# A hybrid encoder layer on one core: two more paired weight tiles, the first head's keys and values among them, the gates' chain in fewer places, the steps nine pieces earlier, and seven vector additions handed to adding transfers

## The reference

```python
xn = rmsnorm(x)
q, k, v, o, ig, fg, u, gates = split(xn @ w_in)      # 8200 output columns
# branch A: 4 heads x 256, chunks of 64 tokens
ig = ig + b_i;  lf = log_sigmoid(fg + b_f)
for each chunk: bcum = cumsum(lf); m_tok = running max; w = exp(logd - m_tok)
    s = (q @ k.T) * w;  num = s @ v + inter * (q @ C);  C = decay * C + (w_last * k).T @ v
ya = (rmsnorm(h) * sigmoid(o)) @ w_proj_a
# branch B
c = causal_dwconv(u[:, :1024] * sigmoid(u[:, 1024:]), width 31)
yb = silu(layernorm(c)) @ w_proj_b                   # mean and variance over all 1024 channels
x = x + rmsnorm((sigmoid(g_A) * ya + sigmoid(g_B) * yb) @ w_out)
x = x + rmsnorm(ffn(x))                              # up, conv of width 3, gelu, down
```

## Time and profile before

| | before |
|---|---|
| median of 3 runs | 1919.84 us (1919.48 to 1921.33) |
| profiled execution | 1919.55 us |
| its span, first to last instruction | 1917.8 us |
| mean granted clock | 0.996 |
| PE busy | 1889.2 us, 99% of the span |
| DVE busy | 1355.3 us, 71% |
| ACT busy | 859.7 us, 45% |
| POOL busy | 84.9 us, 4% |

### The profile page before, as it was taken

How to read it: one execution, slowest core, us unless ns; L and a number is a source line. 1 busy time by engine, 2 the same in 40 slices (tenths; PEclk the granted TensorE clock), 3 DMA queues, 4 the chain that set the end, 5 groups by cost and what they waited for, 6 DMA issues and landing times.

```text
span 1917.8 us, 33091 instructions
## 1 busy us (share of the span) xinstructions
PE 1889.2 (99%) x13241; PEld 1864.8 (97%) x13241; DVE 1355.3 (71%) x2078; ACT 859.7 (45%) x1609; POOL 84.9 (4%) x136
## 2 busy tenths in 40 slices
PE   9999999999998999999999999999999999999997
PEld 8999999999998999999999999999999999999997
DVE  7798999899997646664444468976777676646363
ACT  5554444444424556542122355654454444635342
POOL 0010001000111111110000000000000000000000
PEclk9999999999999999999999999999999999999999
DMA  3445445455354645559131323221222122556654
GB/s 134 141 119 138 135 131 148 109 159 183 103 141 124 192 129 176 153 153 346 45 138 44 127 74 106 90 80 68 86 72 80 68 90 102 190 196 213 208 173 153
DMA packets 117031, 255.09 MB, mean 133 GB/s; under 512 B 19980, under 2 KB 59660, under 8 KB 116880
## 3 DMA queue, kind: packets, MB, share of 16 engines
q1 hardware_dynamic: 105936, 223.10, 33.9%
q0 software_dynamic: 10944, 29.89, 8.1%
HBM read 191.44 MB, written 61.51 MB: 132 GB/s over the span
## 4 chain that ended last, share of the span: by engine, by line
PE 86%; DVE 11%; issue 1%; ACT 1%; DMA 1%; SPq 0%; POOL 0%; DVEq 0%; ACTq 0%; POOLq 0%
PE ps L1155 9%; PE ps L1157 9%; PE ps L1156 9%; PE ps L1519 7%; PE ps L1517 7%; PE ps L1518 7%; PE ps L1319 6%; PE ps L1320 6%; PE ps L1321 6%; PE ps L1535 4%; PE ps L1537 4%; PE ps L1536 4%; DVE cacc L2402 3%; PE ps L1247 2%; PE ps L1244 1%; DVE f_d L2402 1%
## 5 line engine op out<-in xcount | busy, mean ns | idle before, releaser
L1155 PE MATMUL ps<-rx,fhi 128*128 128x364 f32 (+2 forms) x832 | 281.1, 338 | 2.3 <-ACT qkv L1679 2.0
L1156 PE MATMUL ps<-rx,fhi 128*128 128x364 f32 (+2 forms) x832 | 270.2, 325 | 0.0
L1157 PE MATMUL ps<-rx,flo 128*128 128x364 f32 (+2 forms) x832 | 270.1, 325 | 0.0
L1319 PE MATMUL ps<-rx,ahi 128*128 128x304 f32 (+1 forms) x608 | 175.6, 289 | 0.7 <-DVE v L2522 0.7
L1535 PE MATMUL ps<-ghi,dhi 128*128 128x384 f32 (+1 forms) x528 | 173.2, 328 | 2.4 <-DVE glo L2872 1.7
L1320 PE MATMUL ps<-rx,ahi 128*128 128x304 f32 (+1 forms) x608 | 175.3, 288 | 0.0
L1321 PE MATMUL ps<-rx,alo 128*128 128x304 f32 (+1 forms) x608 | 175.2, 288 | 0.0
L1536 PE MATMUL ps<-glo,dhi 128*128 128x384 f32 (+1 forms) x528 | 172.2, 326 | 0.0
L1537 PE MATMUL ps<-ghi,dlo 128*128 128x384 f32 (+1 forms) x528 | 172.2, 326 | 0.0
L2865 DVE TENSOR_TENSOR dlo<-draw,dhi 128x1408 fp32r<-128x1408 f32 x48 | 77.7, 1624 | 121.8 <-ACT dhi L2095 121.8
L1155 PEld LDWEIGHTS ps<-rx,fhi 128*128 128x128 f32 x832 | 157.2, 189 | 4.4 <-ACT qkv L1679 2.6
(11 more groups left out here) (362 smaller groups left out, 5620.4 us busy)
## 6 DMA issues: line engine op xcount, KB each, us to landing
draw<-wdn SPq DMA_DIRECT2D x48, 704.0 KB, 4.2
uraw<-wts SPq DMA_DIRECT2D x44, 512.0 KB, 4.4
araw<-wts SPq DMA_DIRECT2D x76, 256.0 KB, 3.0
fraw<-wts SPq DMA_DIRECT2D x27, 512.0 KB, 3.8
scr_g<-cva SPq DMA_DIRECT2D x22, 512.0 KB, 2.6
qkv<-scr_qkv SPq DMA_DIRECT2D x18, 544.0 KB, 7.2
alo<-wts POOLq DMA_DIRECT2D x38, 256.0 KB, 5.2
fhi<-wts POOLq DMA_DIRECT2D x19, 512.0 KB, 7.3
```

The costliest lines, as they stand in the source:

```text
L1155: pe.matmul(b, hi[:, w], src[:, his[k], cols], start=(k == 0), stop=False)
L1156: pe.matmul(b, hi[:, w], src[:, los[k], cols], start=False, stop=False)
L1157: mm = pe.matmul(b, lo[:, w], src[:, his[k], cols], start=False, stop=(k == KB - 1))
L1319: pe.matmul(b, ahi[s][:, c], bhi[:, k, :], start=(fresh and k == 0), stop=False, skip_group_check=True)
```

## The change

- Two tiles more go in pairs: k0 and v0 (each with its second tile) leave the plain tiles and become pairs 13 and 15, so there are 21 pairs and 54 plain pieces. `PAIRS_B` has another order at its end. Head 0's keys and values then go to DRAM with the others and are loaded back by `load_first_head` at `GATE_END`+3; PE's first scores wait for that too (`qk_in`).
- Steps begin at `S_B`+13 for `S_B`+22. The gates' chain moves up: scans +5 to +4, exponents +6 to +5, the three exponentials +8, +9, +10 to +7, +7, +8, `drow` +11 to +9, its store +12 to +9, `decs` +14 to +10, `gate_turn` +13 to +10, `gate_columns` +17 to +11, the load of head 1 +18 to +13.
- The convolution does 16 instructions a pair for 15, 330 of 408 by the end of the pairs for 282, then 4, 0 or 3 a piece until piece 27. In the last pair eight of them stand behind two evacuations.
- `PASS2` stands in pieces 37, 39, 42, 44, 46, 50, 51, 52 of 54; the last rest (`c_rest`) stands behind the loop.
- `s1` is no longer added by DVE: SP loads `a21` a second time, into the slot of `s1` (behind the load of `a12`, product 1 of the pair ahead being done), POOL adds `a22` by a transfer, and DVE waits for that before `s2`. The blocks 1 to 6 of the convolution are added to `csum` by POOL's transfers from `scr_c`; DVE keeps block 0 (a copy) and block 7 (an addition).

```diff
 PAIRS_B = [("u", 2), ("k", 1), ("v", 1), ("u", 3), ("q", 1), ("k", 2), ("u", 4), ("v", 2), ("q", 2), ("u", 5), ("k", 3),
-           ("v", 3), ("g", 0), ("u", 6), ("q", 3), ("g", 1), ("u", 7), ("g", 2), ("g", 3)]
+           ("v", 3), ("k", 0), ("u", 6), ("v", 0), ("g", 0), ("u", 7), ("q", 3), ("g", 1), ("g", 2), ("g", 3)]
...
-STEP_AT = [S_B + 22 + i for i in range(len(STEPS))]
+STEP_AT = [S_B + 13 + i for i in range(len(STEPS))]
...
-PASS2 = {FULL[S_B + at]: k for k, at in enumerate((CONV_END + 11, CONV_END + 13, 50, 52, 54, 59, 60, 61))}
+PASS2 = {FULL[S_B + at]: k for k, at in enumerate((CONV_END + 10, CONV_END + 12, 42, 44, 46, 50, 51, 52))}
...
+            def first_sum(i):
+                sp.dma_start(araw[aslot(i, 5)][:, :], wts[W_B + 2 * i + 1][:, 0:512]).then_inc(a_s1, 16)
...
+            def load_first_head():
+                for x in range(2):
+                    sp.wait_ge(spl_out[x], 16 * V0_STORES[x][NB])
+                sp.wait_ge(v1_out, 16 * V1_STORES[NB])
+                sp.wait_ge(grp_done, b_at(NB - 1, 3, 1))
+                for b in range(4):
+                    sp.dma_start(qkv[0][:, b, :], scr_qkv[0, b]).then_inc(qk_in, 16)
...
+            def first_sum(i):
+                pool.wait_ge(a_s1, 16 * (i + 1))
+                pool.dma_start(araw[aslot(i, 5)][:, :], wts[W_B + 2 * i + 1][:, 512:1024], accum_op=ALU.add).then_inc(a_s1_sum, 16)
+
+            def add_sum(j):
+                pool.wait_ge(c_sto[j % 2], 32 * (j // 2 + 1))
...
+                    pool.wait_ge(csum_in, 32 * (j - 1))
+                pool.dma_start(csum[:, 0:SEQ], scr_c[j][:, 0:SEQ], accum_op=ALU.add).then_inc(csum_in, 16)
+                pool.dma_start(csum[:, AS0:AW], scr_c[j][:, SEQ:T], accum_op=ALU.add).then_inc(csum_in, 16)
...
-                if s == GATE_END + 13:
+                if s == GATE_END + 10:
                     gate_turn()
...
             def pair_sums(i, last=False):
...
-                dve.tensor_tensor(s1, a21, a22, ALU.add).then_inc(asum, 1)
-                dve.wait_ge(asum, 4 * i + 1)
                 dve.tensor_tensor(a21, a11, a21, ALU.subtract).then_inc(asum, 1)
+                dve.wait_ge(a_s1_sum, 16 * (i + 1))
                 dve.tensor_tensor(s2, s1, a11, ALU.subtract).then_inc(asum, 1)
```

More of the change, by code:

```diff
@@ L67, in in_tiles @@
     return (pair(0) + pair(1) + one("o", 0, 1)
-            + [("gate", 0)] + head(0, "kvq")
+            + [("gate", 0)] + head(0, "q")
             + [(kind, m) for m in range(4, KB) for kind in ("ga", "gb")] + one("o", 1, KB))
@@ L135, in rest_of @@
     return n + 1 + (OPS if n >= N_A else 0)
-TAPS_AT = [6, 12, 27, 42] + [50 + 15 * i for i in range(NB - 4)] + [282]
+TAPS_AT = [6, 12, 27, 42] + [50 + 16 * i for i in range(NB - 4)] + [330]
 assert len(TAPS_AT) == NB + 1
@@ L762, in store_v1 @@
                         sp.wait_ge(c22_set, 2 * i + 2)
-                    to = scr_qkv[k - 1, 2 * "kvq".index(kind) + 1]
+                    to = scr_qkv[k, 2 * "kvq".index(kind) + 1]
                 sp.dma_start(to, v1[:, :]).then_inc(v1_out, 16)
@@ L779, in store_v0 @@
                         sp.wait_ge(c12_set, 2 * i + 2)
-                    to = scr_qkv[k - 1, 2 * "kvq".index(kind)]
+                    to = scr_qkv[k, 2 * "kvq".index(kind)]
                 sp.dma_start(to, v0[i % 2][:, :]).then_inc(spl_out[i % 2], 16)
+            def load_first_head():
[5 more added lines that the diff above has]
+                    sp.dma_start(qkv[0][:, b, :], scr_qkv[0, b]).then_inc(qk_in, 16)
             def load_head(h):
                 if h == 1:
-                    for x in range(2):
-                        sp.wait_ge(spl_out[x], 16 * V0_STORES[x][NB])
-                    sp.wait_ge(v1_out, 16 * V1_STORES[NB])
                     sp.wait_ge(gt_set, 4)
@@ L1106, in a_rest @@
                     .then_inc(a_acc[prod], 16)
+            def first_sum(i):
[3 more added lines that the diff above has]
+                pool.wait_ge(c_sto[j % 2], 32 * (j // 2 + 1))
+                if j == 1:
+                    pool.wait_ge(csum_set, 1)
+                else:
+                    pool.wait_ge(csum_in, 32 * (j - 1))
+                pool.dma_start(csum[:, 0:SEQ], scr_c[j][:, 0:SEQ], accum_op=ALU.add).then_inc(csum_in, 16)
+                pool.dma_start(csum[:, AS0:AW], scr_c[j][:, SEQ:T], accum_op=ALU.add).then_inc(csum_in, 16)
             for i in range(NB):
+                first_sum(i)
                 a_rest(i, 2), a_rest(i, 4)
+                for j in range(1, KB - 1):
+                    if STORE_PAIR.get(j) == i - 1:
+                        add_sum(j)
             pool.wait_ge(grp_done, b_at(NB - 1, 3, 1))
@@ L1132, in _ @@
                     pool.tensor_tensor(sm[p][:, 6:7], sm[p][:, 4:5], eps[:, 1:2], ALU.pow).then_inc(rs_set, 1)
+                for j, at in STORE_SLOT.items():
+                    if s == at + 2 and j < KB - 1:
+                        add_sum(j)
+                if s == S_B + 1:
+                    for j in range(1, KB - 1):
+                        if STORE_PAIR.get(j) == NB - 1:
+                            add_sum(j)
                 if is_last(s) and SLOTS[s][0][0] not in ("mu", "var"):
@@ L1707, in a_hi @@
                 if prod in (5, 6, 7, 3):
-                    act.wait_ge(asum, 4 * i + (4 if prod == 3 else 3))
+                    act.wait_ge(asum, 3 * i + (3 if prod == 3 else 2))
                 act.activation(ahi[s][:, :], araw[s][:, :], ACT.Copy).then_inc(w_hi, 1)
@@ L1712, in a_minus @@
                 s = aslot(i, prod)
-                act.wait_ge(asum, 4 * i + (4 if prod == 2 else 3))
+                act.wait_ge(asum, 3 * i + (3 if prod == 2 else 2))
                 act.wait_ge(w_hi, a_at(i, prod))
@@ L2457, in deviations, with c_rest @@
                     dve.tensor_tensor(cdev[:, t0:t0 + w], c16[:, at:at + w], stat[:, t0:t0 + w], ALU.subtract).then_inc(xc_set, 1)
+            def c_rest(j):
+                if j is not None:
+                    dve.wait_ge(c_hi, j + 1)
+                    dve.tensor_tensor(rz[:, C_HI[j] + 1, :], fz[:, C_HI[j] + 1, :], rz[:, C_HI[j], :].bitcast(F32),
+                                      ALU.subtract).then_inc(c_lo, 1)
             def row_variances():
@@ L2542, in pairs @@
                     else:
-                        some_taps(t0, t1)
+                        some_taps(t0, t1 if i + 1 < NB else t1 - 8)
                     if STORE_PAIR.get(0) == i:
```

105 lines of the change are left out of this document (57 added, 48 removed).

## The result

The changed kernel takes 1931.56 us (median of 4 runs, 1930.23 to 1932.21) and the kernel before 1919.8: a ratio of 1.0057, 95% interval 1.0041 to 1.0073. It is slower by 11.8 us where 1918.2 was forecast. The profiled execution took 1932.21 us, with a span of 1930.3.

The account below looks back on a forecast made before the run. PE, busy 99% of the span, was taken as the bound; against 1919.55 us, -5.6 - 8.3 - 2.3 + 7.5 + 2.3 + 5.0 = -1.4 gave 1918.2 us, range 1911.0 to 1925.5.

Parts of the forecast that it names:

- I count from the end of the pairs: Gates' chain: PE reaches the first scores 51.4 us after the pairs, against 89.35 before; decays' copies done at 58.1 or 60.8.
- the unforeseen: Causes not thought of, counted within the 0.19 chance of slower than 1923.7 us and left out of the range.
- The pairs: Two more pairs cost 42.3 us at 21.15 each, the 12 plain pieces that go save 47.9: -5.6 us.
- the 0.7 of before: PE's wait of 0.7 us in a pair of the old kernel, forecast to vanish.
- Cost 0: First sum s1 by POOL's adding transfer: costs PE nothing at the median landing.
- its worst case: First sum: at the worst landing of the adding transfer, 2 to 3 us lost in one pair.
- about as it is wanted: First sum lands 12.0 to 12.1 us into a pair, at most 14.8; DVE formed it earliest at 11.2.
- the rival's 10 us: Rival: pairs' adding transfers land in 10 us, not 5.2, making s2 late, 1942 us in all; chance 0.07.
- The gates' chain: PE waits 6.7 to 9.4 us at gate_turn and the first scores, taken as +7.5, plus 2.3 of clock.
- Projection B: At its start PE waits 1.75 and 3.25 us for blocks 6 and 7: +5.0, no clock charged.
- The removed waits: Waits of 5.6 (second step's scores), 2.0 (head 0's k and v) and 0.7 (a pair) go: -8.3, and -2.3 of clock.
- Block sums by transfer: Only block 7's addition waits for them: cost 0, up to 2 us if POOL's weights come late.

Follow-up runs that it names:

- a_ring: The kernel after, with the plain tiles' three weight buffers in another turn behind the pairs, so no last-pair product uses the gate tile's: 1923.04 us, 1.0010.
- b_ring: The kernel before with the same other turn of the three weight buffers, putting the gate tile on slots of the last pair's products 6 and 2: 1926.53 us, 1.0031.
- r_best: r_all plus r_quiet's lighter traffic around the broadcast and SP's wait for the last output-gate store moved to the one load needing it: 1914.47 us, 0.9968.
- r_gate: a_ring with ACT's third exponential one place up and DVE's copy of the decays two places up: 1917.92 us, 0.9987.
- a_reload: The kernel after, with SP's two reloads of rx moved ahead of its wait for the gate tile's weight buffer: 1926.6 us, 1.0032.
- r_tail: a_ring with DVE's and ACT's work on the last three normalised blocks in another order: 1922.37 us, 1.0012.
- r_quiet: r_gate with nb loads ahead of the drow wait, the cb load behind the broadcasts and POOL's addition of block 6 five places later: 1917.64 us, 0.9983.
- r_all: a_ring with both moves of the gates' chain (third exponential, decays' copy) and r_tail's order: 1916.89 us, 0.9983.

## Why the prediction was wrong, step by step

**The step that failed** is the one that joins two of its parts: "I count from the end of the pairs". It took for granted that the gate tile begins when the pairs end, as it did before. No wait was looked for at that seam, because no moved instruction stands there. What moved was a number: the product for which SP waits ahead of the gate tile's weights, and behind that wait stood the reload of half of the activations. It cost 7.07 us and 2.3 of clock, 9.4 of the 14.0 us between forecast and profiled execution. Three runs show it: undone in two ways in the kernel after, and made in the kernel before. The forecast gave no chance to it by name; only "the unforeseen" stood above the range.

**The pairs** gain what was forecast and cost 1.5 us more, +43.1 for +41.6. Half of it are PE's waits for DVE's evacuations: 0.8 us, where the forecast had removed the 0.7 of before and put nothing in their place. "Cost 0" for the first sum was the wrong size. In the kernel after, the adding transfers landed a little faster than those of the earlier trace rows (one line's landings, L1124):

```profile
DMA to landing us min/median/max: 3.7/4.5/6.8
```

but DVE waited for them in six pairs, and behind DVE stood the evacuations that PE needs (waits of DVE, L2526 the subtraction behind the new wait):

```profile
DVE araw L2526 <- DMA araw<-wts: 13.1, 6, 2.9
```

The two pairs of runs with and without it put the price at 1.7 us and 2.5 us in their traces, all the traces together at 1.4. The mechanism was named and its worst case written down; "about as it is wanted" should have been read as a cost in those pairs in which it is wanted early. The Trainium skill, "SBUF — State Buffer", on SBUF's two separate sides, says that a transfer issued by GpSimd can be held while VectorE runs an operation in its two-port mode. This trace shows no such hold: the transfers landed in 3.7 to 6.8 us beside a busy VectorE, and the rival's 10 us never came. Whether VectorE's work here is in that mode no run tells, so the rule is not tested by it.

**The gates' chain** was forecast at 6.7 to 9.4 and taken at 7.5; it was 8.48. Its parts in the kernel a_ring, where next to nothing (0.9 us) stands ahead of the gate tile: the copy of `drow` 48.1 us behind the end of the pairs (47.3 forecast), the decays at 60.2 (57.6). The queues on DVE and ACT came out within 1 us; the broadcast landed in 6.6 to 6.9 us each (one line's landings, L886, in the kernel after) and not in the 3.8 of the earlier trace rows; the 4.5 that the forecast allowed at most was too little as well:

```profile
DMA to landing us min/median/max: 6.6/6.8/6.9
```

**Projection B** was forecast as waits of 1.75 and 3.25; they were 1.69 and 2.90. Charging no clock there was wrong: PE's two waits had three matmuls between them, and the clock fell, 2.6 us, which the forecast had kept for its range. With the waits at 0.17 and 0.51 us it didn't fall.

**The removed waits** of 5.6 and 2.0 us are gone from the trace as forecast, the 0.7 in the pairs is not (0.8 after). Block sums by transfer show up in no wait of PE; they were not taken apart by a run of their own.

The causes that the forecast named came out within 1.5 us each, clock at projection B apart; the one that it lacked was larger than any of them.

## What to carry to other kernels

Where the count of anything that goes round a ring changes (pairs, tiles, buffers), evaluate every wait constant that is computed from it, before and after, and look at what is queued behind those waits: the diff shows none of it. When a wait is removed, ask what it was hiding: here a wait for a store, which held for 9 us loads that did not need it, a late broadcast and a full DVE queue each took back part of a repair. An addition moved from an engine to a transfer isn't free when the engine must wait for its landing: 0.69 us of DVE time a pair, hidden, was exchanged for up to 0.1 us a pair that was not. And a profiled execution is one of several: look where it lies among the others, and at its mean clock, before its waits are taken for those of the median.

## What the runs showed of the hardware

- A stall costs more than its length. Behind waits of 5.6, 7.07 and 8.48 us PE's granted clock stood at 1.2 GHz for a while, worth 2.2 to 2.3 us each; behind 5.07 (b_ring) and 4.2 us (r_best) the window reads 0.50 too. Length alone doesn't tell when: behind 3.10 us in r_gate the windows stay at 1.00, behind 2.33 us in a_reload they read 0.75 and 0.82, behind 2.23 us in r_tail 0.74, and behind 1.69 and 2.90 us with three matmuls between (kernel after) 0.50 and 0.79. What else decides was not tried.
- The same four small broadcasts landed in 3.8 us (median, before), 6.8 (after), 4.4 in r_quiet, and in 4.6 to 9.2 in r_all, with a DMA share of 0.95 and 1.06 in the two windows behind 572 us. The runs of r_all spread over 9 us and those of r_best over 2. The mean clock goes with that spread, 0.997 in the fastest runs of r_all and 0.994 in three of the four slowest, so the clock stood low for longer in these; that late landings are the reason is likely and was not shown.
